# Four output tiles behind each norm take x one chunk at a time, the embedding's projection moves into the norms' gaps, and norms are broadcast by a product with the identity

## The reference

```python
def rms(x, g):
    return x * lax.rsqrt(jnp.mean(x * x, axis=-1, keepdims=True) + EPS) * g

def hybrid_layer(x, ...):                     # two of these
    proj = rmsnorm(x, norm_g) @ w_in          # q, k, v, forget gate of branch a; latents of b; q, k, v of c; gates
    y_a = causal_block_attention(..., log_cum)          # log_cum: running sum of log sigmoid forget gates
    cq, ckv = rmsnorm(b_cq, g_cq), rmsnorm(b_ckv, g_ckv)      # 384 and 256 wide
    y_b = causal_block_attention(cq @ w_uq with rope, ckv @ w_ukv, ...)
    y_c = sliding_window_sink_attention(...)
    return x + sum_of_gated_branches @ w_out

def second_block(x, p, ...):                  # x: the first block's output, normed
    h = x
    for i in range(2):
        hn = rms(h, g_mix_pre[i])
        y = mixer_ab(hn, ...) if i == 0 else mixer_c(hn, ...)
        h = h + rms(y, g_mix_post[i])
        hn = rms(h, g_mlp_pre[i])
        y = jnp.square(jax.nn.relu(hn @ w_mlp_in[i])) @ w_mlp_out[i]       # 1024 -> 4096 -> 1024
        h = h + rms(y, g_mlp_post[i])
        gate = jax.nn.sigmoid(h @ w_ple_gate[i])
        h = h + gate * (p[i] @ w_ple_proj[i])                              # p[i]: 512 x 256
    return h
```

## Time and profile before

| | us |
|---|---|
| median of 3 runs | 3145.75 |
| the runs | 3149.0, 3143.48, 3145.75 |
| the profiled execution | 3146.51 |
| its span | 3144.7 |
| PE busy | 2896.0 (92%) |
| DVE busy | 1625.8 (52%) |
| ACT busy | 1226.1 (39%) |
| POOL busy | 161.2 (5%) |
| mean granted TensorE clock | 0.941 |

### The profile page before, as it was taken

One profiled execution on the slowest core, in us unless ns is written; L12 is line 12 of the kernel. 1 busy time (PEld: TensorE's weight loads), 2 busy tenths in 40 slices (PEclk: granted clock), 3 DMA queues, 4 the chain that ended last, 5 costly groups with the idle time before them and its releaser, 6 DMA issues.

```text
span 3144.7 us, 39975 instructions
## 1 busy us (share of the span) xinstructions
PE 2896.0 (92%) x15368; PEld 2400.7 (76%) x15368; DVE 1625.8 (52%) x3359; ACT 1226.1 (39%) x2659; POOL 161.2 (5%) x123
## 2 busy tenths in 40 slices
PE   7999998999999998999797979999998799799998
PEld 7888988899888777777565658888775477588886
DVE  6455545555455554545546453344666754534445
ACT  3335434433234434433546433333443244333333
POOL 2000000001000000000100030000110000200000
PEclk9999999999999999999798979999997589799999
DMA  3201112122211212122121013322221010132322
GB/s 123 72 24 61 53 43 68 48 74 88 81 48 33 75 42 74 54 71 91 52 77 34 24 36 98 101 94 95 80 78 47 0 44 29 55 99 94 101 91 91
DMA packets 116127, 207.84 MB, mean 66 GB/s; under 512 B 13920, under 2 KB 23008, under 8 KB 115808
## 3 DMA queue, kind: packets, MB, share of 16 engines
q1 hardware_dynamic: 114784, 201.09, 20.2%
q10 hardware_dynamic: 1152, 4.20, 0.3%
HBM read 203.07 MB, written 2.10 MB: 65 GB/s over the span
## 4 chain that ended last, share of the span: by engine, by line
PE 77%; DVE 14%; ACT 6%; issue 2%; POOL 0%; DMA 0%; DVEq 0%; POOLq 0%; SPq 0%; ACTq 0%
PE pp L1695 20%; PE pp L1697 19%; PE pp L1696 19%; PE pp L1747 5%; PE pp L1771 5%; PE pp L1759 2%; DVE wl L1301 2%; ACT tmp L1192 2%; PE pp L1691 1%; PE pp L1693 1%; PE pp L1692 1%; DVE Hl L1320 1%; PE pp L1804 1%; PE pp L1715 1%; ACT wh L1124 1%
## 5 line engine op out<-in xcount | busy, mean ns | idle before, releaser
L1695 PE MATMUL pp<-Hh,wh 128*128 128x512 f32 (+1 forms) x2322 | 892.8, 384 | 119.7 <-DVE wl L1301 54.2
L1696 PE MATMUL pp<-Hl,wh 128*128 128x512 f32 (+1 forms) x2322 | 820.2, 353 | 0.0
L1697 PE MATMUL pp<-Hh,wl 128*128 128x512 f32 (+1 forms) x2322 | 819.1, 353 | 0.0
L1301 DVE TENSOR_TENSOR wl<-raw,wh 128x512 fp32r<-128x512 f32 (+2 forms) x780 | 533.2, 711 | 421.1 <-ACT wh L1124 419.8
L1695 PEld LDWEIGHTS pp<-Hh,wh 128*128 128x128 f32 x2322 | 456.5, 197 | 236.6 <-DVE wl L1301 67.7
L1124 ACT ACTIVATE wh<-raw 128x512 fp32r<-128x512 f32 (+2 forms) x780 | 450.7, 606 | 245.3 <-PE pp L1697 185.7
L1696 PEld LDWEIGHTS pp<-Hl,wh 128*128 128x128 f32 x2322 | 458.9, 198 | 57.1 <-issue 8.7
L1697 PEld LDWEIGHTS pp<-Hh,wl 128*128 128x128 f32 x2322 | 456.7, 197 | 55.8
L1695 PE MATMUL pp<-Yh,wh 128*128 128x512 f32 (+1 forms) x1280 | 481.8, 376 | 5.3 <-DVE Yl L1318 4.3
L1696 PE MATMUL pp<-Yl,wh 128*128 128x512 f32 (+1 forms) x1280 | 459.0, 359 | 0.0
L1697 PE MATMUL pp<-Yh,wl 128*128 128x512 f32 (+1 forms) x1280 | 459.0, 359 | 0.0
(11 more groups left out here) (212 smaller groups left out, 2680.9 us busy)
## 6 DMA issues: line engine op xcount, KB each, us to landing
raw<-in_w SPq DMA_DIRECT2D x710, 256.0 KB, 2.7
raw<-in_w SPq DMA_DIRECT2D x38, 192.0 KB, 2.4
raw<-in_w SPq DMA_DIRECT2D x32, 128.0 KB, 2.0
out<-X SPq DMA_DIRECT2D x8, 256.0 KB, 2.0
con<-in_con ACTq DMA_DIRECT2D x1, 1576.0 KB, 12.2
X<-in_x SPq DMA_DIRECT2D x2, 528.0 KB, 6.1
X<-in_x ACTq DMA_DIRECT2D x2, 528.0 KB, 7.3
Z<-in_p ACTq DMA_DIRECT2D x2, 512.0 KB, 3.3
```

The costliest lines, as they stand in the source:

```text
L1301: e.tensor_tensor(part("wl", j), landing(j), part("wh", j).bitcast(F), ALU.subtract).then_inc(*dve.up("split", j))
L1695: e.matmul(it.ps, wh, xh, start=it.first, stop=False)
L1696: e.matmul(it.ps, wh, xl, start=False, stop=False)
L1697: e.matmul(it.ps, wl, xh, start=False, stop=it.end).then_inc(*pe.up())
```

## The change

1. **Norms.** No diagonals are built. The column of 1/rms is broadcast as the stationary operand (stride 0) against the identity. The sums are made in two parts, `norm_total` over POOL's running total and `norm_col` over the last square; `whole` is gone. Squares rotate through three places, so from the fourth on ACT's square waits for POOL's add of the square before. The rows use bank NB.
2. **chunk_major and lead.** Four output tiles are made together: one panel now holds one chunk of x for all four, and the four tiles' steps of a chunk follow each other. `lead` runs all 32 steps of the four tiles, 4 steps of a fifth, the norm's column, 2 more steps, the rows, and then the four evacuations in a row. It stands in `first_layer` (gates and one or two tiles of q), `mixer_ab`, `mixer_c` and the first round of `mlp`; `ple` makes its tiles 0 to 3 in this way.
3. **Embedding.** p is loaded before `second_half` and split at its fifth tile. Projections 0 to 3 lie in `mix_end` (two around the norm, two after its rows), 4 to 7 in the same way at the end of `mlp`.
4. **add_normed.** All eight adds of x are on DVE.

```diff
-    def norm_begin(tiles, squares="K", first=0, at=0):
-        return dict(tiles=tiles, at=at, squares=squares, first=first, c=first, begin=mark(), bank=free[NB])
+    def norm_begin(tiles, width=D, squares="K", first=0, at=0):
+        base = tiles[0][0]
+        n = tiles[-1][1] - base
+        slots = [m[squares][:, T * x:T * x + n] for x in range(first, first + 3)]
+        return dict(tiles=tiles, base=base, at=at, width=width, slots=slots, c=0, begin=mark(), squares=[])
...
+    def norm_total(N):
+
+        N["total"] = do("norm_total", tiles=N["tiles"], at=N["at"], base=N["base"], free=free[NB], sq=N["slots"][0], square=N["squares"][0],
+                        added=N.get("added"))["n"]
+
+    def norm_col(N, col):
+        if "total" not in N:
+            norm_total(N)
+        n = do("norm_col", tiles=N["tiles"], at=N["at"], base=N["base"], width=N["width"], sq=N["last"], square=N["squares"][-1], col=col)["n"]
+        N["column"], N["col"] = n, col
+        free[NB] = ("act", "norm_col", n)
 
     def norm_rows(N, rs):
-        bks = [next_bank() for _ in N["groups"]]
-        n = do("norm_rows", tiles=N["tiles"], groups=N["groups"], dg=N["dg"], rs=rs, banks=[bank(b) for b in bks],
-               free=[free[b] for b in bks], col=N["col"])["n"]
+        tiles, base = N["tiles"], N["base"]
+        parts_ = [tiles[:1], tiles[1:]] if tiles[0][1] - tiles[0][0] < 128 else [tiles]
+        bks = [next_bank() for _ in parts_[1:]] + [NB]
+        n = do("norm_rows", parts=[[(i + x, p - ts[0][0], q - ts[0][0]) for i, (p, q) in enumerate(ts)] for x, ts in enumerate(parts_)],
+               rows=[rs[:, ts[0][0] - base:ts[-1][1] - base] for ts in parts_], banks=[bank(b) for b in bks], free=[free[b] for b in bks],
+               col=N["col"], column=N["column"])["n"]
         for b in bks:
             free[b] = ("act", "norm_rows", n)
-        return ("act", "norm_rows", n)
-
-    def lead(N, rs, first, second, first_n=1, second_n=1):
-        for k in range(8 * first_n):
-            next(first)
-        n = N["tiles"][-1][1] - N["tiles"][0][0]
-        sqs = [m[N["squares"]][:, T * x:T * x + n] for x in (N["first"], N["c"] - 1)]
-        N["whole"] = do("whole", sqs=sqs, square=N["square"])["n"]
-        norm_col(N, D, col)
-        for k in range(8 * second_n):
-            next(second)
+
+    def chunk_major(name, idx, tiles, x, kc, ready):
+
+        outs, at, every = [], 0, []
+        for cs, ranges, evac in tiles:
+            outs += [(at, len(cs), a, b, next_bank(), evac) for a, b in ranges]
+            at += len(cs)
+            every += cs
+        g = pieces["n"]
+        for k in range(kc):
+            [(_, j)] = panel(name, idx, [k], every)
+            begin_panel(j)
+            for at, n, a, b, bk, _ in outs:
+                do("step", ps=bank(bk)[0:n, 0:b - a], j=j, i=0, cols=(at, at + n), x=x[k], a=a, b=b, first=k == 0, end=k == kc - 1,
+                   free=free[bk] if k == 0 else None, ready=known(ready[k]), group=(g, bk))
+        yield
+        for at, n, a, b, bk, evac in outs:
+            free[bk] = evac(bank(bk)[0:n, 0:b - a], a, b, ("pe", "group", g, bk))
+
+    def lead(N, rs, several, then, n):
+
+        next(several)
+        then = then()
+        for _ in range(n):
+            next(then)
+        norm_col(N, col)
+        for _ in range(n // 2):
+            next(then)
         norm_rows(N, rs)
-        run(first)
-        run(second)
+        run(several)
+        run(then)
...
-        gates = win([*(list(cols(1536, 8)) * 8), *cols(B0 + 640, 32), *swapped(B0 + 640)], TOKR, fgate)
-        lead(N, rs, gates, qk(Q, 0, 0, QR), 2, len(QR))
+        some = 2 if l else 1
+        gates = [([*(list(cols(1536, 8)) * 8), *cols(B0 + 640, 32), *swapped(B0 + 640)], TOKR, fgate)]
+        heads = [(list(cols(128 * c, 128)), QR, two_heads(Q, 2 * c, rs, before)) for c in range(some)]
+        lead(N, rs, chunk_major("w_in", l, gates + heads, Hx, 8, hr), lambda: qk(Q, 0, some, QR), 4 * len(QR))
         filled = do("ones rows", q=Q[64:66, :, :], k=K[64:66, :, :], before=before, gates=mark())["n"]
         forget = mark()
-        run(qk(Q, 0, 1, QR))
+        rest = [(Q, 0, c, QR) for c in range(some + 1, 4)] + [(K, 512, c, TOKR) for c in range(4)]
...
-        norm_sum(Nk)
-        norm_sum(Nq)
-        Nk["sum"] = Nq["sum"]
-        norm_col(Nk, 256, col2)
-        norm_col(Nq, 384, col3)
+        norm_col(Nk, col2)
+        norm_col(Nq, col3)
         zgate(B0 + 672, 1)
...
+    def norm_and_project(N, project, c0, before):
+
+        norm_total(N)
+        run(project(c0, before))
+        norm_col(N, col)
+        run(project(c0 + 1, before))
         norm_rows(N, rsS)
+        left = [project(c0 + 2, before), project(c0 + 3, before)]
+        for steps in left:
+            for k in range(2):
+                next(steps)
+        return left
...
-            f = do("add_normed", y=y[:, c, :], x=X2[:, c, :], g=sm[:, g + c:g + c + 1], rs=rsS, pool=c % 2 == 1, began=began)["n"]
-            then(c, ("pool" if c % 2 else "dve", "add_normed", f))
+            f = do("add_normed", y=y[:, c, :], x=X2[:, c, :], g=sm[:, g + c:g + c + 1], rs=rsS, began=began)["n"]
+            then(c, ("dve", "add_normed", f))
         caught_up()
...
+            if f == 0:
...
+                lead(N, rsS, chunk_major("w_mlp_in_2", i, [(of(c), ALLR, evac_up(c)) for c in range(4)], Hx, 8, hr), lambda: up(4), 4)
+            for c in range(0 if f else 5, 8):
...
+        run(chunk_major("w_ple_gate_2", i, tiles[:4], Hx, 8, hr))
+        for cs, ranges, evac in tiles[4:]:
+            run(gemm_steps(panel("w_ple_gate_2", i, K8, cs), Hx, 8, ranges, hr, evac))
...
+        lead(N, rsS, chunk_major("w_in_ab_2", 0, [(list(cols(128 * c, 128)), ALLR, rotated(Q, 0, c)) for c in range(4)], Hx, 8, hr),
+             lambda: gemm_steps(panel("w_in_ab_2", 0, K8, cols(512, 128)), Hx, 8, ALLR, hr, rotated(K, 0, 0)), 4)
+        for c in range(1, 4):
+            run(rotary(K, 0, c, 512))
...
+        lead(N, rsS, chunk_major("w_in_c_2", 0, [(list(cols(128 * c, 128)), ALLR, low(c)) for c in range(4)], Yx, 8, yr),
+             lambda: win(cols(512, 128), low(4)), 4)
+        norm_col(norms["q"], col2)
...
+        for part, ps, free in zip(it.parts, it.banks, it.free):
             if free:
                 pe.wait_ge(*free)
-        for i, (p, q) in enumerate(it.tiles):
-            ps = it.banks[0 if i == 0 else -1]
-            at = p - it.tiles[len(it.groups) - 1 if i else 0][0]
-            e.matmul(ps[:, at:at + q - p], m["con"][0:q - p, ONES:ONES + 128], it.dg[i], start=True, stop=True).then_inc(*pe.up("norm_rows", it.n))
+            for i, p, q in part:
+                e.matmul(ps[:, p:q], it.col[:, i:i + 1].to_broadcast([128, 128]), m["con"][:, IDENT:IDENT + q - p], start=True, stop=True).then_inc(
+                    *pe.up("norm_rows", it.n))
```

More of the change, by code:

```diff
@@ L202, in norm_chunk @@
     def norm_chunk(N, src, by):
-        c, first = N["c"], N["first"]
+        c = N["c"]
         N["c"] += 1
-        n = N["tiles"][-1][1] - N["tiles"][0][0]
[L206 to L227, removed]
@@ L229, in norm_rows @@
-    def norm_rows(N, rs):
-        bks = [next_bank() for _ in N["groups"]]
-        n = do("norm_rows", tiles=N["tiles"], groups=N["groups"], dg=N["dg"], rs=rs, banks=[bank(b) for b in bks],
-               free=[free[b] for b in bks], col=N["col"])["n"]
+        slots = N["slots"]
+        to = slots[0 if c == 0 else 2 - c % 2]
+        N["last"] = to
+        n = do("square", src=src, to=to, by=by, begin=N["begin"] if c == 0 else None,
+               add=(slots[0], slots[2 - (c - 1) % 2]) if c > 1 else None, squared=N["squares"][-1] if c > 1 else None,
+               given=N["squares"][-1] if c > 2 else None)["n"]
@@ L930, in evac @@
                 return f
-            return win(cols(128 * c, 128), evac)
-        lead(N, rsS, low(0), low(1))
-        run(low(2))
-        run(low(3))
-        norm_col(norms["q"], 384, col2)
-        run(low(4))
+            return evac
+        lead(N, rsS, chunk_major("w_in_c_2", 0, [(list(cols(128 * c, 128)), ALLR, low(c)) for c in range(4)], Yx, 8, yr),
+             lambda: win(cols(512, 128), low(4)), 4)
+        norm_col(norms["q"], col2)
         norm_rows(norms["q"], rs2S)
@@ L1028, in schedule @@
     caught_up()
-    hr, N = mixer_ab(hr, N)
-    hr = mlp(0, hr, N)
+    hr, N, *p = mixer_ab(hr, N)
+    hr = mlp(0, hr, N, *p)
     hr, N = ple(0, hr)
-    hr, N = mixer_c(hr, N)
-    hr = mlp(1, hr, N)
+    hr, N, *p = mixer_c(hr, N)
+    hr = mlp(1, hr, N, *p)
     ple(1, hr)
@@ L1635, in square @@
             e.tensor_tensor(total, total, one, ALU.add).then_inc(*pool.up("square", it.n))
-    def whole(it):
-        pool.wait_ge("pool")
-        pool.wait_ge("act", "square", it.square)
-        total, one = it.sqs
-        e.tensor_tensor(total, total, one, ALU.add).then_inc(*pool.up("whole", it.n))
     def ones_rows(it):
@@ L1699, in step, with norm_total @@
```

(10 more changed lines are left out.)

169 lines of the change are left out of this document (91 added, 78 removed).

## The result

The changed kernel takes 3202.85 us in the median of four runs (3190.24 to 3210.87), the kernel before 3147.38 of its four runs by then; the ratio is 1.017, with a 95% interval of 1.0125 to 1.0216. It is slower, as forecast, by 55 us where 43 were forecast. Its eight runs in the study, with the four of the first experiment, lie in two groups: 3188 to 3195 (five) and 3208 to 3211 (three). The forecast of 3189 is the time of the first group; what makes the second is a stretch at the low clock that the forecast had no place for.

The account below looks back on a forecast made before the run. PE, busy 92% of the span, was taken as the bound, with only its waits for other engines able to give time back. Terms summed to +43 on 3146.51, forecasting a median of 3189 us, range 3152 to 3215.

Parts of the forecast that it names:

- The point on which it turned: chunk_major: splits for chunks 2 to 7 queue behind add_normed, so PE does 8 steps during the phase and 24 remain.
- The mlp's lead: Both mlps: five evacuations before the needed split make PE wait 7.2 us instead of 0.98; +5.5 each net, +11.
- the pause costs 1.7 at the low clock: Behind each mlp lead's wait PE runs at a lower granted clock, losing 1.7 us; with the wait +7.9.
- the 2.4 taken off for the norm: add_normed in mix_end: DVE's 24 operations take 23.3 instead of 24.2 us, begun 1.3 to 1.5 earlier: -2.4.
- Ple and mixer_c: First ple: wait of 10.4 us, +9 net of 3.2 saved; mixer_c's lead +4; second ple +1.5.
- mixer_ab: Its lead: rows some 15 us later, rotary evacuations strictly one after another, PE waits some 24 us; +10.5.
- Latent norms: First two layers: the second norm's total waits for bank NB until ACT has read the first's sums; +5 for both.
- the unknown terms: Latent norms 0 to 5.4, pauses 1.7 to 2.7, mixer_c 0 to 6, mixer_ab 5 to 13; said to give 3168 to 3204.
- R1: Rival, faster: DVE and ACT drain the evacuations before PE uses its 10 steps, only savings remain; 3135, chance 0.15.
- R2: Rival, half absorbed: places bound by DVE and ACT absorb PE's lateness; +22, 3168, chance 0.18.
- R3: Rival, heavier: five pauses cost 2.7 us of clock each, ten evacuation operations slow beside POOL; +15, 3204, chance 0.12.
- The table load: mix_end: square root's load behind the first projection's evacuation; the skill page's drain adds 1.4 us at two places, the trace nothing.

Follow-up runs that it names:

- the first experiment: The changed kernel run again with no edit: 3188.45, 3194.18, 3194.81 and 3207.76 us, ratio 1.0166 to the kernel before.
- second profile: Profile of the changed kernel run again with no edit; span 3192.3 us, against 3209.0 in its earlier profile and 3144.7 for the kernel before.

## Why the prediction was right, and where it was off

**The point on which it turned** was right. Chunks 2 to 7 were not taken as they came: 12.97 us of idle PE stand in `mix_end`'s phase before the split of chunk 2,

```profile
1925.66 0.79 PE L1744 MATMUL pp<-Hh,wh 128*128 128x512 f32 x1 [12.97 <-DVE wl L1364]
```

which begins only when DVE is through with x. Counted with their phases (the two rows of the table together), the mlps lost 16.1 us in the changed kernel; with the evacuations spread they lost 0.2, and with the steps written inside the phase besides they gained 6.4, 3 us each. So most of the loss was the order of evacuations and splits behind the phase, and the chunks that follow x are worth 3 us an mlp.

**The mlp's lead.** Wait 7.12 for 7.2. The stage cost 9.4 us on average for a forecast of 7.9. A term that was too small is "the pause costs 1.7 at the low clock": the 14 us behind the wait have a granted clock of 0.79, which costs 2.9,

```profile
1943.90:1957.90 14.00, 13.99 (x49) 0.79 0.33 99
```

and it is 0.80 in the second mlp, 0.82 in ple and 0.78 in mixer_ab (second profile), 2.5 to 3.1 us each.

Of the 2.4 taken off for the norm nothing came on balance. The phase was shorter by 1.4 (forecast 0.9), but it began later, not earlier: in the changed kernel the last square ends at 1891.47 + 0.63 = 1892.10 and the first scaling is at 1901.81, 9.7 us; before it is 7.8 from the table load to the scaling. The end of `add_normed` came 0.5 us later, where a sign of being right was to be 2 earlier. The step that failed is "begun 1.3 to 1.5 earlier". In the second profile the phase begins 1.9 us later in the first `mix_end` and 3.3 in the second, so that the two leads with their phases cost 18.9 - 2.8 + 1.9 + 3.3 = 21.3 us there, for a forecast of 11. Between the square and the scaling stand the projection's evacuation ahead of the table load (1894.21) and two splits ahead of the first scaling (1900.60); that these are the cause is argued, not tried.

**Ple and mixer_c.** Wait 9.04 for 10.4, ple and lead +18.8 for 16.1. Most of the error is in mixer_c (6.2 for 4). The phase at the mlps' ends gave 5.0 for 3.2 in the first and 4.8 for about 2 in the second, so the last ple's +1.5 came out at -3.2 with its phase.

**mixer_ab.** +12.4 for 10.5; the rows came 16.1 us later for "some 15", and the chain is the bound, as said.

**Latent norms.** The term was mis-sized: +10 for 5. I had bounded it by what ACT does (one load and the roots) and left out that the second norm's own sums, 4.5 us at the low clock, come behind it instead of beside it. An edit that makes two things take turns costs the whole second thing, not the hand-over.

**Not foreseen.** The rest of the layers gave 6.4 us back in the second profile. Of these 2.6 are the final norm, from the last square to the first scaling 4.29 for 6.85 (no diagonals, half the sums), which the forecast had counted in mixer_ab. The others are mostly one spot: before, PE waits 2.58 us for a bank that DVE had not evacuated (1374.50) and loses clock behind it, in all kernels with the new norms it does not. The norms' rows no longer take a bank from the rotation, so each later tile falls on another one; that this is the reason is argued. And the long stretch in the attention, 18 us where it was profiled: three of the eight runs of the changed kernel lie as much higher, and with two of them among its first four the median is 14 us above the forecast.

**How near the sum was, and luck.** The second profile is 47.6 us over before, for 43. That is so near because errors cancelled: the mlps' leads cost 10 us more than forecast, the latent norms 5, ple with mixer_c 2.7 and mixer_ab 1.9. Against them the rest of the first two layers with the final norm gave back 6.4 us that the forecast didn't have, the ends of the mlps with the last ple gave 6.4 more than it had (-9.7 and +1.6 for -3.2 and +1.5), and layer 0's lead cost 1.5 less. The total is in part luck; the waits behind the evacuations are not. One sum in the forecast is also wrong by itself: the unknown terms as listed, each taken at both ends, give 3174.5 to 3199, not 3168 to 3204.

**The rivals.** R1 is refuted: evacuations did not drain in time. R2, absorption, is refuted where it matters: nothing of latent norms, mixer_ab or ple was taken back behind them; only layer 0's lead cost 0.5 us instead of 2. R3's number (3204) came out by another cause. One half of its mechanism is there: a long pause costs 2.5 to 3.1 us of clock, as it said, and not 1.7. The other half is not: the five evacuations of an mlp's lead take 0.68 or 0.69 us for their scaling, none is slowed by POOL.

**The table load.** The changed kernel's square root in `mix_end` begins at 1896.12, 0.02 us behind a load that ends at 1894.82 + 1.28 = 1896.10, and the load begins 0.01 us behind the evacuation ahead of it (1894.21 + 0.60). The drain of 1.38 us that the Trainium skill ("ScalarE: Activation LUTs", section "What ACT_TABLE_LOAD costs") adds to a switch does not show here either.

## What to carry to other kernels

Read how far ahead the operands of the next product are prepared, and where that preparation stands in its queue: a loop order that lets a product follow its producer wins nothing while its weight splits are written behind the producer, and costs what it bunches behind it. Write the consumer's steps between the producer's where the producer is followed by cheap evacuations (a gain of 3 us an mlp, 9 in the last ple, phases counted in and evacuations spread); where a serial chain of evacuations is the bound, start that chain early instead. And price a shared bank by everything that has to take turns on it.

## What the runs showed of the hardware

The same program ran the same attention at a granted clock of 0.61 over 48 us in one execution and at 0.96 in another, 18 us apart, with PE busy nearly all of that time in both (46.90 and 46.55 of 48 us). Busy time in the profile therefore does not say that PE does as much: a matmul of this stretch takes 46.90 / 149 = 0.31 us on average in the long one and 0.20 in the other. Differences under some 20 us between variants had to be read stretch by stretch.
